# Inversion of the triangular factors in a fused three-block decoder kernel: VectorE adds both groups of a level and then turns them, and ScalarE copies T before it moves halves across

## The reference

```
def step(state, inp):
    r_t, w_t, k_t, v_t, kk_t, a_t = inp
    sa = jnp.einsum('bhvk,bhk->bhv', state, -kk_t)
    state = (state * w_t[:, :, None, :]
             + sa[..., None] * (kk_t * a_t)[:, :, None, :]
             + v_t[..., None] * k_t[:, :, None, :])
    y_t = jnp.einsum('bhvk,bhk->bhv', state, r_t)
    return state, y_t
```

## Time and profile before

| | |
|---|---|
| median of three timed runs | 2441.29 us (2440.8 to 2442.96) |
| profiled execution: its time, its span | 2441.39 us, 2439.5 us |
| TensorE busy (share of the span) | 2414.7 us (99%) |
| VectorE busy | 1610.4 us (66%) |
| ScalarE busy | 1200.4 us (49%) |
| POOL busy | 114.0 us (5%) |

### The profile page before, as it was taken

The page is one execution under the profiler, slowest core; times in us unless marked ns, Lnnn a source line. Parts: engine busy times, 40 slices in busy tenths (PEclk is TensorE's granted clock), DMA queues, the critical chain, the costliest instruction groups (busy, mean ns, idle before and its releaser), DMA issues.

```text
span 2439.5 us, 50836 instructions
## 1 busy us (share of the span) xinstructions
PE 2414.7 (99%) x21762; PEld 2365.8 (97%) x21762; DVE 1610.4 (66%) x1912; ACT 1200.4 (49%) x1688; POOL 114.0 (5%) x68
## 2 busy tenths in 40 slices
PE   8999999999999999999999999999999999999999
PEld 8999999999999999999999999999999999999987
DVE  6666667748556498586576545587666666666684
ACT  5444455545344484464455334554444444443564
POOL 0000000003600002002100000000000000000000
PEclk9999999999999999999999999999999999999999
DMA  6444444354555564352444555455555555555543
GB/s 240 159 162 162 155 142 162 137 179 165 184 190 181 182 235 157 106 190 89 158 154 156 219 183 188 173 195 189 181 183 187 189 189 184 182 185 188 207 173 138
DMA packets 59092, 425.57 MB, mean 174 GB/s; under 512 B 6576, under 2 KB 6704, under 8 KB 8400
## 3 DMA queue, kind: packets, MB, share of 16 engines
q1 hardware_dynamic: 58464, 421.68, 48.1%
q0 software_dynamic: 496, 1.90, 0.2%
HBM read 419.23 MB, written 4.33 MB: 174 GB/s over the span
## 4 chain that ended last, share of the span: by engine, by line
PE 94%; DVE 3%; ACT 1%; DMA 1%; issue 0%; DVEq 0%; SPq 0%; ACTq 0%
PE banks L244 27%; PE banks L246 27%; PE banks L245 26%; PE banks L298 2%; PE banks L2376 1%; PE banks L2378 1%; PE banks L300 1%; PE banks L2377 1%; PE banks L299 1%; DVE weights_lo_sb L207 1%; DMA raw_weights_sb<-weights 1%; PE banks L573 1%; PE banks L760 1%; PE banks L776 0%; PE banks L1470 0%
## 5 line engine op out<-in xcount | busy, mean ns | idle before, releaser
L244 PE MATMUL banks<-xa_hi_sb,weights_hi_sb 128*128 128x256 f32 (+3 forms) x4290 | 1218.9, 284 | 11.2 <-DVE xa_lo_sb L337 9.9
L246 PE MATMUL banks<-xa_hi_sb,weights_lo_sb 128*128 128x256 f32 (+3 forms) x4290 | 1209.2, 282 | 0.0
L245 PE MATMUL banks<-xa_lo_sb,weights_hi_sb 128*128 128x256 f32 (+3 forms) x4290 | 1207.3, 281 | 0.0
L207 DVE TENSOR_TENSOR weights_lo_sb<-raw_weights_sb,weights_hi_sb 128x1024 fp32r<-128x1024 f32 x786 | 934.4, 1233 | 261.7 <-ACT weights_hi_sb L186 256.1
L186 ACT CAST weights_hi_sb<-raw_weights_sb 128x1024 fp32r<-128x1024 f32 x786 | 779.9, 1047 | 558.4 <-DMA raw_weights_sb<-weights 557.9
L244 PEld LDWEIGHTS banks<-xa_hi_sb,weights_hi_sb 128*128 128x128 f32 x4290 | 806.5, 188 | 15.2 <-issue 12.4
L245 PEld LDWEIGHTS banks<-xa_lo_sb,weights_hi_sb 128*128 128x128 f32 x4290 | 809.2, 189 | 0.2
L246 PEld LDWEIGHTS banks<-xa_hi_sb,weights_lo_sb 128*128 128x128 f32 x4290 | 807.5, 188 | 0.0
L244 PE MATMUL banks<-xb_hi_sb,weights_hi_sb 128*128 128x256 f32 (+1 forms) x688 | 196.6, 286 | 0.6 <-DVE o_sb L1042 0.3
L246 PE MATMUL banks<-xb_hi_sb,weights_lo_sb 128*128 128x256 f32 (+1 forms) x688 | 195.0, 283 | 0.0
L245 PE MATMUL banks<-xb_lo_sb,weights_hi_sb 128*128 128x256 f32 (+1 forms) x688 | 194.8, 283 | 0.0
(11 more groups left out here) (462 smaller groups left out, 2272.8 us busy)
## 6 DMA issues: line engine op xcount, KB each, us to landing
raw_weights_sb<-weights SPq DMA_DIRECT2D x393, 1024.0 KB, 4.8
h_sb<-h SPq DMA_DIRECT2D x4, 544.0 KB, 8.3
h_aside<-h_sb SPq DMA_DIRECT2D x1, 2176.0 KB, 9.1
h_sb<-h_aside SPq DMA_DIRECT2D x1, 2176.0 KB, 9.7
out<-y_sb SPq DMA_DIRECT2D x4, 512.0 KB, 2.7
conv_gate_sb<-ple_gain POOLq DMA_DIRECT2D x1, 512.0 KB, 5.0
conv_value_sb<-ple_gain POOLq DMA_DIRECT2D x1, 512.0 KB, 7.9
masks_sb<-consts_rw POOLq DMA_DIRECT2D x1, 448.0 KB, 5.6
```

The lines of the kernel that those rows point to most:

```text
L207: dve.tensor_tensor(c.w_lo[n % RAW][:, half], c.raw[n % RAW][:, half], c.w_hi[n % RAW][:, half].bitcast(F32), ALU.subtract).then_inc(c.sem ...
L244: pe.matmul(out, w_hi[:, k, a], x_hi[:, tile, cols], start=begin, stop=False)
L245: pe.matmul(out, w_hi[:, k, a], x_lo[:, tile, cols], start=False, stop=False)
L246: done = pe.matmul(out, w_lo[:, k, a], x_hi[:, tile, cols], start=False, stop=end)
```

## The change

On VectorE the loop over the two groups is split: both additions come first, and then, with the same waits on `inverse_ready`, both turnings. On ScalarE the copy of T comes ahead of the two crossing copies of the same group, with its wait on `tm_done` ahead of that on `turn_ready`. No instruction that works on data is added or taken away, and TensorE's and POOL's queues stay as they are.

```diff
--- before.py
+++ after.py
@@ -1614,14 +1614,14 @@
         for level in range(1, 6):
             for g in range(2):
                 v = 2 * (5 * b + level - 1) + g + 1
+                act.wait_ge(S("tm_done"), v)
+                act.copy(t["tt"][:, 8 * g:8 * g + 8, :].rearrange("p (k u) i -> p k (u i)", k=2),
+                         ps[:, 2 * g:2 * g + 2, 0:256]).then_inc(S("t_ready"), 1)
                 act.wait_ge(S("turn_ready"), v)
                 odd = t["xx"][:, 8 * g:8 * g + 8, :].rearrange("p (x j) i -> p x j i", j=2)[:, :, 1, :]
                 for q in range(2):
                     m = act.copy(t["crossed"][64 * q:64 * q + 64, 4 * g:4 * g + 4, :], odd[64 - 64 * q:128 - 64 * q])
                 m.then_inc(S("cross_ready"), 1)
-                act.wait_ge(S("tm_done"), v)
-                act.copy(t["tt"][:, 8 * g:8 * g + 8, :].rearrange("p (k u) i -> p k (u i)", k=2),
-                         ps[:, 2 * g:2 * g + 2, 0:256]).then_inc(S("t_ready"), 1)
             if level == 1:
                 split_hi(c, act, n + 17)
             if level == 3:
@@ -1804,7 +1804,8 @@
                 dve.wait_ge(S("inverse_done"), v)
                 dve.tensor_tensor(y_of(p), y_of(p), ps[:, 2 * p:2 * p + 2, 0:256].rearrange("p j (x i) -> p x j i", x=CHUNKS),
                                   ALU.add).then_inc(S("inverse_ready"), 1)
-                dve.wait_ge(S("inverse_ready"), v)
+            for p in range(2):
+                dve.wait_ge(S("inverse_ready"), 2 * (5 * b + level - 1) + p + 1)
                 if level < 5:
                     turn(p)
         split_lo(c, dve, n + 19)
```

## The result

The changed kernel takes 2445.27 us (median of 22 runs, 2444.28 to 2447.45), the kernel before 2441.43 (22 runs, 2440.38 to 2443.25): 3.8 us more, ratio 1.0016 with a 95% interval of 1.001 to 1.0022. The forecast was 2444.4, 3.1 us more.

What follows compares the result with a forecast made beforehand. TensorE, busy 99% of the span, was taken to bound the kernel, so only its waits count. Removed waits of -2.2 us and new ones of +5.3 gave +3.1 on 2441.29, hence 2444.4 us, range 2440.5 to 2447.0.

Steps and rivals of the forecast that it cites:

- The new wait: TensorE before group 1 of L1478, held by ScalarE's last crossing pair: 0.53 us in each of ten levels, +5.3 us.
- T + 0.76: ScalarE's chain of six copies starts 0.76 us after T, the start of a level's L1470 on TensorE.
- The gain: TensorE's six waits at L1470 for VectorE's second addition go, 0.36 us each: -2.2 us.
- I + 0.76: Add 0 starts on VectorE 0.76 us after I, the start of a level's second block L1478.
- about 0.8: Sign in the changed profile: VectorE's two additions about 0.8 us apart, with the turnings behind them.
- Feedback: The new wait moves group 1's products, add 1, turnings and next level's start alike by 0.53 us; the gain stands.
- The casts had their cover: ScalarE's weight casts after levels 1, 3 and 5 end before the next level's copy of T, 0.4 us left.
- it costs nothing: POOL's masking starts earlier and its end is asked for later, so it adds no time.
- A: Rival: ScalarE's chain is shorter than its spacings say, no wait replaces the removed one: 2439.1 us, chance 7%.
- B: Rival: add 1 is still late for L1470, only the loss stands: 2446.6 us, chance 6%.
- C: Rival: turn 0 reaches ScalarE late and holds group 0's pair and everything behind it: 2446.4 us, chance 4%.
- D: Rival: ten new waits make TensorE's clock fall from 2.4 to 1.2 GHz for a while: 2453.8 us, chance 1%.

Runs made afterwards that it cites:

- e2: Kernel before with ScalarE's part alone, copy of T ahead of the crossing pair in both groups: 2444.84 us against 2440.91.
- e1: Kernel before with VectorE's part alone, both additions and then both turnings: 2442.46 us against 2440.91.
- e5: Changed kernel with five kept tiles behind L1470 and one behind L1478 (two in levels 3 and 5): 2452.05 us against 2441.41.
- e7: Changed kernel with four kept tiles behind L1470, one between L1478's groups, one behind (two in levels 3 and 5): 2448.91 us against 2441.41.
- e4: Kernel before with ScalarE's copy of T ahead of the crossing pair in group 1 only: 2440.91 us against 2440.91.
- e6: Kernel before with kept tiles three behind L1470, one between L1478's groups, two behind (three in levels 3 and 5): 2442.95 us against 2441.41.
- e9: Kernel before with one kept tile moved from in front of L1478 to behind it, levels 1, 2 and 4 only: 2439.99 us against 2441.84.
- e3: Kernel before with ScalarE's copy of T ahead of the crossing pair in group 0 only: 2445.21 us against 2440.91.
- e8: Kernel before with one kept tile moved from in front of L1478 to behind it in all levels: 2440.83 us against 2441.41.

## Why the prediction was right

**The new wait** was the term that decided, and its place, cause and number were as forecast: ten waits in front of group 1 of L1478, the chain starting at T + 0.76 and ending at T + 3.65. Its size was 0.57 us, not 0.53: ScalarE's last copy to TensorE's weight load is 0.06 us, not 0.05, and the rest lies inside the block: its group 1 was loaded 0.55 us late and the block became 0.57 longer. Over ten levels that is 0.4 of the 0.7 us between +3.1 and the measured +3.8. The inversions alone grew by 3.6, and the remaining 0.2 is inside the spread of the runs.

**The gain** of 2.2 us came: of the six blocks of L1470 at 1.52 us five went to 1.16 and one to 1.29, none with a wait in the view. But I credited it to VectorE's order, and e2 shows that it comes without it. A wait of 0.57 us on one side of a level's circle pays for a lateness of 0.36 on the other. The sum was right because the wait goes either way and was counted once; the reason given for its going was not the one that was needed. To that extent the number was lucky. Alone, VectorE's order does remove the wait (e1) and gives back more than it gains through ScalarE's pair. The additions lie 1.03 us apart. The prediction's own times, I + 0.76 and I + 1.75, give 0.99; the "about 0.8" among its signs didn't follow from them.

**Feedback** was worked out rightly for the changed kernel, where every level has the same wait. In e1 it makes the waits alternate, which I had not foreseen.

**What lost nothing** was right in its result. The casts had their cover, turn 0 had time, and the masking began earlier and ended in time. But "it costs nothing" for POOL looked only at when the masking ends. It left out what the masking meets on its way. It starts 0.22 us behind VectorE's split, much as before the change (0.19), and had it started ahead of it, each such level would have cost VectorE up to 2.2 us (3.43 - 1.18 in e5), and TensorE's loads 0.5 to 0.8 us of idle time in front of L1470 (e5, e7). The trace of the kernel before had a case of it, outside the inversions:

```profile
1045.43 2.62 DVE L207 TENSOR_TENSOR weights_lo_sb<-raw_weights_sb,weights_hi_sb 128x1024 fp32r<-128x1024 f32 x1
```

```profile
1044.59 2.39 POOL L1866 TENSOR_TENSOR y_sb<-rw_tile_sb 128x1024 f32<-128x1024 f32 x1
```

POOL's instruction is first by 0.84 us and ends at 1046.98, and the split ends 1.1 us behind it, as in e5.

**The rivals.** A, the shorter chain: refuted, the spacings were 0.61, 0.85 and 0.61 again. The Trainium skill's overlap of about 93 ns ("ScalarE: Activation LUTs", "What ACT_TABLE_LOAD costs") showed between the casts. It also shows, by about 0.1 us, between a copy of T and a cast right behind it (963.80, 0.58 us, then 964.28 in the earlier trace rows), and in e4 between two copies of T of 0.59 us each, though the program has a wait between them:

```profile
963.97 1.07 ACT L1627 COPY y_sb<-banks 128x512 f32<-128x512 f32 x2 [3.33 <-PE banks L1470]
```

Beside the crossing copies it is missing, and in the changed kernel a crossing pair lies behind every copy of T. So a wait between two instructions, one of the two reasons that the prediction gave, doesn't by itself keep them apart; why the crossing copies don't overlap, no run shows.

B, the gain not coming, and C, turn 0 too late, both fell with the rows above; C is the mechanism of e1, not of the changed kernel. D: the clock stayed at 0.999.

## What to carry to other kernels

Where engines go round in a circle, level after level, work that one of them does early beside another's block is worth its place: before moving anything ahead of it, write down from when the whole chain of copies can start, not only how long each is. A wait of that circle is paid once. If one side waits, lateness on the other costs nothing up to the length of that wait. So price both orders alone before adding their parts up, and look first at moving a piece of filling work from one side of the circle to the other, which here shortened the inversions by 1.5 us where both new orders together made them 3.6 longer. And when an edit moves the start of POOL's instruction by tenths of a microsecond, look at which VectorE instruction it now comes before.

## What the runs showed of the hardware

- VectorE's subtraction with two inputs in SBUF (128 x 1024, 1.18 us alone) and POOL's multiplication (128 x 1024, 2.41 us when it is first) exclude each other, and the one that starts second waits for the other. Split first by 0.22 us (968.20, changed kernel): masking 3.19 us, its end 2.23 us behind the split's. Masking first by 0.06 us (e5): split 3.43 us, its end 1.08 behind the masking's. Within some hundredths the recorded starts don't tell who wins: in e7 the masking stands 0.02 us ahead once (967.68, the split 967.70), and yet it was the one that waited, with 3.45 us for a split of 1.19. The Trainium skill ("SBUF — State Buffer", "Terms") has this as a lock held for the full instruction, with the loser blocked entirely; the traces agree to 0.1 us where the split waits and to 0.2 us where the masking does.
- VectorE's addition, which has one input in PSUM, isn't held: in level 1 of the changed kernel the masking ran from 963.15 to 966.24, and the addition within it, at 965.35, took its usual 0.69 us.
- One group of three 128 x 256 matmuls between blocks of 64 x 64 ones costs TensorE 0.37 us over its own time (e6).
- An operand that comes late inside a block of small matmuls costs about 0.1 us more than the idle time that the weight loads show: 0.57 us for 0.45 idle (changed kernel), 0.36 for 0.27 (before), 0.22 for 0.10 (e5, level 1), and 0.13 where the view shows no idle time at all (e9).
- TensorE's weight load follows 0.06 us behind the end of ScalarE's crossing pair, and 0.11 to 0.12 behind the end of its copy of T out of PSUM (e1, e3, e8).
